# Transformer stack on one core: the memory norm moved under the second inverse transform, and one gate tile instead of two

## The reference, cut to what matters

```python
u = _rms_norm(h, norm_mix_g); proj = u @ w_in
hy = _short_conv_centred(proj[..., :HY_COLS], ...)         # 12 tiles of 128 columns
z, g1, g2 = hy split in three
for o, gate in enumerate((g1, g2)):                        # two long convolutions, by transforms
    conv = irfft(rfft(z, 1024) * spec[:, o])[:, :L]
    z = gate * (conv + z * skip[o])
y_hy = _group_rms_norm(z, hy_norm_g, 8)
# mLSTM: 16 gate columns, log_f = log_sigmoid(f); F = cumsum(log_f), forward and backward
y_ml = _mlstm_bidirectional(q, k, v, o_pre, gates, ml_gate_b)
h = h + concat([y_hy, y_ml]) @ w_out
h = h + _cross_attention(_rms_norm(h, norm_x_g), _rms_norm(mem, norm_mem_g), wq, wk, wv, wo)
```

## Time and profile before

| what | value |
|---|---|
| median of 3 runs | 2057.27 us (2055.19 to 2059.74) |
| profiled execution, its own time | 2057.35 us |
| its span in the profile | 2055.6 us (1.75 us lie around it) |
| TensorE busy | 1982.7 us (96%), 11602 matmuls |
| VectorE busy | 939.9 us (46%) |
| ScalarE busy | 731.1 us (36%) |
| GpSimd busy | 345.4 us (17%) |
| DMA | 179.68 MB, mean 87 GB/s |

### The profile page before, as it was taken

One profiled execution on the slowest core, in us unless ns is written; L12 is line 12 of the kernel. 1 busy time (PEld: TensorE's weight loads), 2 busy tenths in 40 slices (PEclk: granted clock), 3 DMA queues, 4 the chain that ended last, 5 costly groups with the idle time before them and its releaser, 6 DMA issues.

```text
span 2055.6 us, 27428 instructions
## 1 busy us (share of the span) xinstructions
PE 1982.7 (96%) x11602; PEld 1206.2 (59%) x11602; DVE 939.9 (46%) x1246; ACT 731.1 (36%) x1173; POOL 345.4 (17%) x355
## 2 busy tenths in 40 slices
PE   7999998899999999999999999999999899999997
PEld 5655654666674444886467444448766575444466
DVE  5666686655453332244656222322655554323224
ACT  4443311444444431133435222212465434222213
POOL 1011100110032210014005221101510025121100
PEclk9999999999999999999999999999999899999999
DMA  6211200233313233222121222233111022333331
GB/s 240 82 62 62 83 21 0 103 103 103 103 62 103 103 103 103 103 103 83 62 94 72 84 102 101 103 102 124 62 62 62 21 83 83 103 103 102 103 103 42
DMA packets 28181, 179.68 MB, mean 87 GB/s; under 512 B 2912, under 2 KB 7136, under 8 KB 7136
## 3 DMA queue, kind: packets, MB, share of 16 engines
q1 hardware_dynamic: 27264, 170.93, 24.1%
q10 hardware_dynamic: 512, 4.94, 0.7%
q0 software_dynamic: 288, 2.10, 0.3%
HBM read 175.86 MB, written 2.10 MB: 87 GB/s over the span
## 4 chain that ended last, share of the span: by engine, by line
PE 88%; DVE 8%; ACT 2%; issue 1%; DMA 1%; POOL 0%; ACTq 0%; DVEq 0%; SPq 0%
PE psum_a L381 25%; PE psum_a L383 25%; PE psum_a L382 25%; PE psum_b L514 2%; PE psum_a L703 2%; DVE X L1803 1%; DVE RINV L1777 1%; PE psum_a L641 1%; PE psum_a L714 1%; PE psum_b L618 1%; DVE ARENA L1803 1%; PE psum_a L828 1%; DVE W_PARTS L1783 1%; DVE X L1808 1%; PE psum_b L1039 1%
## 5 line engine op out<-in xcount | busy, mean ns | idle before, releaser
L1783 DVE SCALAR_TENSOR_TENSOR W_PARTS<-W,W_PARTS 128x2048 f16<-128x2048 f32 x145 | 332.5, 2296 | 617.7 <-ACT W_PARTS L1214 617.7
L381 PE MATMUL psum_a<-U,W_PARTS 128*128 128x512 f16 (+1 forms) x1272 | 477.1, 375 | 8.6 <-POOL U L2560 3.9
L382 PE MATMUL psum_a<-U,W_PARTS 128*128 128x512 f16 (+1 forms) x1272 | 477.0, 375 | 0.0
L383 PE MATMUL psum_a<-U,W_PARTS 128*128 128x512 f16 (+1 forms) x1272 | 476.7, 375 | 0.0
L1214 ACT ACTIVATE W_PARTS<-W 128x2048 f16<-128x2048 f32 x145 | 275.7, 1905 | 491.2 <-PE psum_a L383 491.2
L381 PE MATMUL psum_a<-ARENA,W_PARTS 128*128 128x256 f16 (+2 forms) x956 | 295.7, 309 | 3.6 <-DVE W_PARTS L1783 3.0
L382 PE MATMUL psum_a<-ARENA,W_PARTS 128*128 128x256 f16 (+2 forms) x956 | 295.6, 309 | 0.0
L383 PE MATMUL psum_a<-ARENA,W_PARTS 128*128 128x256 f16 (+2 forms) x956 | 295.5, 309 | 0.0
L381 PEld LDWEIGHTS psum_a<-U,W_PARTS 128*128 128x128 f16 x1272 | 124.8, 98 | 154.0 <-DVE W_PARTS L1783 9.4
L383 PEld LDWEIGHTS psum_a<-U,W_PARTS 128*128 128x128 f16 x1272 | 124.9, 98 | 144.2 <-issue 0.8
L382 PEld LDWEIGHTS psum_a<-U,W_PARTS 128*128 128x128 f16 x1272 | 124.8, 98 | 143.5 <-issue 3.2
(11 more groups left out here) (306 smaller groups left out, 2697.6 us busy)
## 6 DMA issues: line engine op xcount, KB each, us to landing
W<-weights SPq DMA_DIRECT2D x159, 1024.0 KB, 4.8
CON<-const ACTq DMA_DIRECT2D x1, 3071.5 KB, 11.7
X<-x_in SPq DMA_DIRECT2D x2, 1024.0 KB, 7.4
U<-dft POOLq DMA_DIRECT2D x1, 1024.0 KB, 5.4
ARENA<-dft POOLq DMA_DIRECT2D x1, 1024.0 KB, 5.3
ARENA<-mem_in ACTq DMA_DIRECT2D x1, 1024.0 KB, 4.8
y_out<-U SPq DMA_DIRECT2D x2, 512.0 KB, 3.0
y_out<-U SPq DMA_DIRECT2D x4, 256.0 KB, 2.2
```

The costliest lines, as they stand in the source:

```text
L381: nc.tensor.matmul(out, left(0), right(0), start=first, stop=False)
L382: nc.tensor.matmul(out, left(0), right(1), start=False, stop=False)
L383: return nc.tensor.matmul(out, left(1), right(0), start=False, stop=last)
L1783: nc.vector.scalar_tensor_tensor(out=home[:, 1, :], in0=W[g % 2][:, :], scalar=W_SCALE, in1=home[:, 0, :], op0=ALU.mult, op1=ALU.subtract) ...
```

## The change

Two edits.

1. The 16 gate columns go into one tile: input gates on rows 0 to 3 and 32 to 35, forget gates on rows 64 to 67 and 96 to 99. TensorE computes one gate tile, in one bank. VectorE reads rows 0 to 63 and then rows 64 to 127 of it into the same rows of `ROWS` as before.
2. `MEM` lies in `EVEN` (the upper half of `U`), which is free once VectorE has read the last transform of the filter, `("spec", 1, 1, 1, 1)`. ScalarE starts the load there, waits for `mirrored` 3 and for the load, squares, and takes the root. TensorE runs `norm_sum("mem", 0)` between the two halves of the second inverse transform. VectorE does reciprocal and gains ahead of the first adds of the out tiles, ScalarE the high parts after the split of panel out+4. GpSimd waits for its own eight low parts of `MEM` before it writes the first low part of x over it. Two small row tiles of the Hyena norm move from `ZT[0], ZT[1]` to `ZT[2], ZT[3]`, since `SQ_REST` lies on the first two.

```diff
-        m = Arena()
-        MEM = m.take(8, N_MEM)
+        m = Arena(8 * N_MEM)
+        MEM = EVEN.rearrange("p a b -> p (a b)").rearrange("p (k t) -> p k t", k=8)
...
-                        for m in range(2):
-                            first_banks[n, m] = reuse(A, ("gate", m) if n == 0 else ("in", 12 + m))
+                        for m in range(1 + n):
+                            first_banks[n, m] = reuse(A, "gate" if n == 0 else ("in", 12 + m))
...
-                        for m in range(2):
+                        for m in range(1 + n):
                             last = product(first_banks[n, m][:, HALVES[half]], lambda l: w[:, l, kt, m * P:(m + 1) * P],
...
                 inverse_transform(o, 0)
                 if o == 0:
                     filters(1, range(3))
+                if o:
+                    norm_sum("mem", 0)
                 inverse_transform(o, 1)
...
-            head_roots("hy", 4, ZT[0:64, 0, :], lambda ct: gback[:, ct, :], B)
+            head_roots("hy", 4, ZT[0:64, 2, :], lambda ct: gback[:, ct, :], B)
...
-            project("out", 8, MIX16, tail="x", middle=lambda: norm_sum("mem", 0), first=2)
+            project("out", 8, MIX16, tail="x", first=2)
...                                             (ScalarE)
+            when_free(act, A, ("spec", 1, 1, 1, 1))
+            act.dma_start(MEM[:, :, :], mem_in).then_inc(sem("mem_landed"), 16)
+            act.wait_ge(sem("mirrored"), 3)
+            act.wait_ge(sem("mem_landed"), 16)
+            squares("mem", 0, in_mem)
+            root("mem", 0)
             for ct in range(4):
                 act.wait_ge(sem("z_gated"), 5 + ct)
...
-            act.wait_ge(sem("hy_low"), 4)
-            act.dma_start(MEM[:, :, :], mem_in).then_inc(sem("mem_landed"), 16)
             used("out", 0)
             used("out", 1)
             split(panel_of["out"] + 4)
-            root_table()
-            act.wait_ge(sem("mem_landed"), 16)
-            squares("mem", 0, in_mem)
-            root("mem", 0)
             for kt in range(KT):
                 high_tile("mem", 0, kt, in_mem, MEM16)
...                                             (VectorE)
             for n, bias in ((0, "gate_bi"), (1, "gate_bf")):
-                key = ("gate", n)
-                when_done(dve, A, key)
-                nc.vector.tensor_scalar(ROWS[0:64, n, :], A.bank(key)[0:64, :], DESCALE, par(bias, p=64), ALU.mult, ALU.add)\
-                    .then_inc(A.freed_sem(key), 1)
+                when_done(dve, A, "gate")
+                at = slice(64 * n, 64 * n + 64)
+                nc.vector.tensor_scalar(ROWS[0:64, n, :], A.bank("gate")[at, :], DESCALE, par(bias, p=P)[at, :], ALU.mult, ALU.add)\
+                    .then_inc(A.freed_sem("gate") if n else sem("input_gates"), 1)
...
+            inverse("mem", 0)
+            gain_tiles("mem", 0, in_mem, in_mem, "norm_mem")
             first, second = arrivals("x")
             for add in first[:4]:
                 add()
             split(panel_of["out"] + 4)
-            inverse("mem", 0)
-            gain_tiles("mem", 0, in_mem, in_mem, "norm_mem")
             for add in first[4:]:
                 add()
...                                             (GpSimd)
             norm_low("mem", in_mem, MEM16)
+            pool.wait_ge(sem("low_mem"), KT)
             norm_low("x", in_qx, U16)
```

More of the change, by code:

```diff
@@ L1398, in _ @@
             centre_tap(13)
-            when_free(act, A, ("gate", 1))
+            when_free(act, A, "gate")
             link(nc.scalar.activation(ROWS[0:64, 2, :], ROWS[0:64, 1, :], ACT.Abs))
@@ L1499, in _ @@
                 nc.scalar.activation(PR[ct], HY[:, ct, :], ACT.Square).then_inc(sem("hy_squared"), 1)
-            root_rows("hy", ZT[0:64, 1, :], 64)
+            root_rows("hy", ZT[0:64, 3, :], 64)
             for ct in range(4):
@@ L2042, in _ @@
             dve.wait_ge(sem("softplus"), 1)
-            when_free(dve, A, ("gate", 1))
+            when_free(dve, A, "gate")
             link(nc.vector.scalar_tensor_tensor(out=ROWS[0:64, 3, :], in0=ROWS[0:64, 1, :], scalar=0.0, in1=ROWS[0:64, 2, :],
@@ L2049, in _ @@
             used("gate", 3)
-            when_free(dve, A, ("gate", 0))
+            dve.wait_ge(sem("input_gates"), 1)
             link(nc.vector.tensor_tensor(ROWS[0:64, 0, :], ROWS[0:64, 0, :], ROWS[0:64, 4, :], ALU.subtract))
@@ L2266, in _ @@
                     used(("og", 1))
-            inverse_rows("hy", ZT[0:64, 0, :], ZT[0:64, 1, :])
+            inverse_rows("hy", ZT[0:64, 2, :], ZT[0:64, 3, :])
             for ct in range(4):
@@ L2719, in _weight_stream @@
     gates = w_in[:, off + 2 * D_ML:]
-    gate_i, gate_f = _np.zeros((2, D, P), _np.float32)
-    gate_i[:, 0:4], gate_i[:, 32:36] = gates[:, 0:4], gates[:, 8:12]
-    gate_f[:, 0:4], gate_f[:, 32:36] = gates[:, 4:8], gates[:, 12:16]
+    gate = _np.zeros((D, PANEL_COLS), _np.float32)
+    for n in range(4):
+        gate[:, (0, 64, 32, 96)[n]:(0, 64, 32, 96)[n] + 4] = gates[:, 4 * n:4 * n + 4]
     conv, value_out = _panels_k8(w_in[:, :off]), _panels_k8(w_in[:, off:off + 2 * D_ML])
-    out = _panels_k8(_np.concatenate([gate_i, gate_f], 1)) + conv[6:] + value_out[:2] + conv[:6] + value_out[2:]
+    out = _panels_k8(gate) + conv[6:] + value_out[:2] + conv[:6] + value_out[2:]
     out += _panels_k8(a["w_out"][0])
@@ L2785, in _params @@
     for name, f, b in (("gate_bi", 0, 8), ("gate_bf", 4, 12)):
-        block = _np.zeros((64, 1), _np.float32)
-        block[0:4, 0], block[32:36, 0] = gb[f:f + 4], gb[b:b + 4]
+        block = _np.zeros((P, 1), _np.float32)
+        at = 64 if f else 0
+        block[at:at + 4, 0], block[at + 32:at + 36, 0] = gb[f:f + 4], gb[b:b + 4]
         put(name, block)
```

## The result

The changed kernel takes 2040.44 us (median of 12 runs, 2035.26 to 2052.14), the kernel before beside it 2057.09 (12 runs, 2054.58 to 2062.41). The ratio is 0.993, 95% interval 0.9917 to 0.9943: 16.6 us less by the medians, 14.4 by the ratio (12 to 17). Predicted were 2041.6 and 2037.5 to 2047.0.

A forecast was written before the change was run, and what follows sets the result against it. TensorE, busy 96% of the span, was taken as the bound, so only less work, less idling or a higher clock pays. 12.9 + 1.8 + 1.0 = 15.7 us off 2057.3 gave 2041.6 us, range 2037.5 to 2047.

The forecast's parts named there:

- both stalls: TensorE's waits: 6.76 us for the memory's squares before the out halves, 4.42 us for the mirror in the second inverse transform.
- Part 1: Out projection: with the memory sum moved away, TensorE's gap between out tile 3 and the halves goes, 12.9 us.
- Each margin: Out halves: panels, banks and squares would be ready 0.3 to 1.4 us before TensorE needs them.
- Part 2: Second inverse transform: the memory sum fits free into the mirror stall and the clock stays up, 1.8 us.
- Part 3: Gate tile: half 1 loses 2.6 us of matmuls, longer idle before 32.5 costs 1.6 in clock, so 1.0 us.
- I take the loss, at 1.6 us: Before the convolution panel: 3.3 us of TensorE idle was expected to bring the clock down, costing 1.6 us.
- rival 2: Gate tile buys only idle time and clock: -0.6 us, time 2043.2; sign: slow clock over 3.2 us behind 32.5; 13%.
- rival 3: Out halves: splits or squares take the stall's place, price 1 to 4 us, time 2042.7 to 2045.6; 12%.
- 1 (late load): Second inverse transform: the memory's load comes late, gain there -0.7 to 1.1 us, time 2042.3 to 2044.1; 10%.
- 4 (the sum blocks the transform): Second inverse transform: the norm sum holds up its second half; 2059 us with a load of 23 us; 3%.

The follow-up runs named there:

- mem_only: The kernel before with the memory's edit alone, both gate tiles kept; 2042.96 us, ratio 0.9938.
- late_gains: The changed kernel with VectorE's reciprocal and gains of the memory back behind its split of panel out+4; 2052.17 us, ratio 0.997.
- late_sum: The changed kernel, memory loaded and squared early, but its norm sum, root, reciprocal and gains back in the out projection; 2051.73 us, ratio 0.9976.
- gate_only: The kernel before with the gate tile's edit alone; 2058.97 us, ratio 1.0007.
- filled_half0: The changed kernel with the second gate tile put back in token half 0 alone, as dead work into an unread bank; 2042.28 us, ratio 0.9918.
- three loads: The changed kernel with two more 1 MB loads ahead of the memory's load, the squares waiting for all three; 2048.24 us, ratio 0.9958.
- filled_all: The changed kernel with the second gate tile in half 0 as dead work and dead matmuls at eight places where TensorE waits; 2029.43 us, ratio 0.987.
- filled_mem: The kernel before with the memory edit alone, plus dead matmuls in TensorE's stalls; 2033.26 us, ratio 0.9887.

## Why the prediction was right, and its one wrong size

**What bounds the kernel.** Right: both stalls stood where the timeline had them, and mem_only, which changes nothing else, has the gain.

**Part 1, 12.9 us.** Right in the trace: the 13.1 us between two starts became 0.21. Each margin held, and by its own steps. VectorE was free of the adds at 371.28 + 1.28 = 372.56, 0.57 us before it could split (I had 0.3), and panel 2 was 0.7 us early, as predicted. Between 376 and 440 TensorE's list of waits has only the 3.0 us for a split that the kernel before has too. The choice that mattered was 3.26 us for the gains and not 5.35, for the reason that GpSimd has nothing to do then. late_gains shows the other figure where GpSimd is at work.

**Part 2, 1.8 us.** Right: 8.86 - 7.17 = 1.7, load 4.7 us (4.8 used), inverse released by the mirror. I had put the issue at 1.56 us behind the start of the first half (328.04 - 326.48), and it came at 331.05 - 329.46 = 1.59. The absolute times are 3 us later than mine, through slow stretches at 31, 244 and 282. late_sum adds that the low clock is worth up to 2.4 there.

**Part 3, 2.6 - 1.6 = 1.0 us.** The step that failed is "I take the loss, at 1.6 us". The idle of 3.2 us (predicted 3.3) and the fall of the clock came as written, and half 1's 2.6 us too. But the stretch at 1.2 GHz covered 24 matmuls and cost 24 x (0.21 - 0.109) = 2.4 us in place of 1.6. My price came from windows of 3.50 and 5.00 us in the earlier trace rows, each of which holds a slow stretch half as long as this one (29.5 to 36.3). So half 1's gain was all but used up by 245: 0.3 us in gate_only's trace. Then gate_only lost more at later, untouched stalls. By its runs part 3 is -1.4 us (-3.3 to 0.4). The edit shows its 2.62 us whole only where the stalls are filled.

The sign that I had named for rival 2 is there: a slow clock for more than 3.2 us behind the panel's start (4.9 us, 31.39 to 36.3). Its price for part 3, -0.6, lies inside the interval, and mine doesn't. I had held it to 13%. The rule of the Trainium skill that I weighed there spoke the right way for the size, but not for the mechanism that I drew from it: the thin half 0 did lift the clock. Its matmuls from 26.10 on stand 0.11 us apart, and the clock fell again in the idle time. Putting the removed matmuls back (filled_half0) kept it up. Why a stall of 1.64 us at 282 takes the clock down in some traces and not in others is open: the runs show it, not its cause. And that the loss at these later stalls comes from the gate edit is not shown.

**Sum.** Parts 1 and 2 gave 14.7 and mem_only has 12.8 (8 to 17). Part 3's error of 2.4 us is less than the spread of either, so the total came out 1.2 us from the prediction. Some of that closeness is luck: of the twelve runs four are 5 to 11 us above it and two 6 below, and the first norm sum alone moves a run by more than 1 us. (A slip of 0.1 in the prediction: rival 3's times begin at 2042.6.)

**Rivals.** 1 (late load): did not occur; with three loads it costs 4.3 us by the medians and 5.7 by the trace. 2 (the gate tile buys only idle time and clock): occurred, inside part 3. 3 (splits, squares): did not occur; forced, it costs 8. 4 (the sum blocks the transform): nowhere near.

## What to carry to other kernels

Price a removed stall by the gap between the last matmul before it and the first behind it, then walk each engine's queue with the times of rows to see what is late next: that was exact to 0.2 us here (14.6 us in the trace for 14.7). Matmuls removed from a stretch that waits for another engine are no gain but a thinner stretch, and can cost the clock of the work behind. When two kernels differ by less than 1%, compare the low-clock time (two times the span times one less the mean granted clock) before comparing anything else, and if TensorE is the bound, fill its known stalls with matmuls into an idle bank: on its own it gave nearly as much as this tuning step, it gave 11 to 15 us more on top of it, and it made 2.6 us measurable. And set two traces to zero at a mark behind the first slow stretch, not at the start of the span.

## What the hardware showed that I had not expected

- The same code behind the same stall ran twice as long at 1.2 GHz in one kernel as in another: 246.7 to 250.1 in the kernel before, 244.5 to 251.3 in the changed one. Over a profiled run, two times the span times one less the mean clock gives about 49 us at 1.2 GHz (before), 70 (after), 28 (mem_only) and 12 (filled_all), each within 2, since the clock has three digits; 70 is 2 x (1 - 0.983) x 2050.3. Half of it is lost time at most, 35 us in the run of 2052.14.
- That figure leaves out the start, where TensorE is slow as well: it left the lower level inside the first norm sum, and that sum's second eight matmuls took 1.89 us in four traces (gate_only is one) and 3.14 in another (filled_mem). This shifts all that follows by up to 1.2 us, ahead of any edit. The Trainium skill, "TensorE: Matmul & The Clock Gate", section "Part 1: The HAM clock gate", says that the count of slow matmuls at a kernel's start varies from run to run, and the traces agree. It also says that the penalty of this ramp is under 1% of a typical kernel's span. That holds for the start here, but the slow stretches behind later stalls come on top: up to 35 of 2050 us, 1.7%, and dead matmuls won back 11 to 15 us.
- One kernel's runs fall into groups through the clock: 2035.3, 2040 and 2050 us for the changed kernel, and time multiplied by clock is the same within 0.2% in all of them.
- Eight gains on VectorE take 3.26 us alone (at 368.10 after) and 5.35 or 5.32 beside GpSimd's low parts (late_gains).

Of all kernels run, filled_all is the fastest: medians of 2029.1 and 2029.4 us, 0.987 of the kernel before.
